# One MLP up product as seven half-size products per pair of output tiles

## The reference, cut to what matters

```python
def _sq_relu_mlp(x, w1, w2):
    return jnp.square(jax.nn.relu(x @ w1)) @ w2     # w1 (1024, 4096), w2 (4096, 1024)
```

## Time and profile before

| what | us |
|---|---|
| median of 3 runs | 2175.79 |
| the runs | 2176.32, 2171.49, 2175.79 |
| span of the profiled execution (first to last instruction) | 2171.2 |
| its own time outside the span | not shown by the page |
| PE busy | 2118.4 (98%) |
| DVE / ACT / POOL busy | 1026.0 / 818.7 / 133.8 |
| output projection, in the chain | 538.97 to 643.5 |
| up product of layer 0 | 644.37 to 1033.26 |
| down product of layer 0 starts | 1033.26 |

### The profile page before, as it was taken

The page is one execution under the profiler, slowest core; times in us unless marked ns, Lnnn a source line. Parts: engine busy times, 40 slices in busy tenths (PEclk is TensorE's granted clock), DMA queues, the critical chain, the costliest instruction groups (busy, mean ns, idle before and its releaser), DMA issues.

```text
span 2171.2 us, 31832 instructions
## 1 busy us (share of the span) xinstructions
PE 2118.4 (98%) x13227; PEld 1912.4 (88%) x13227; DVE 1026.0 (47%) x1503; ACT 818.7 (38%) x1507; POOL 133.8 (6%) x214
## 2 busy tenths in 40 slices
PE   7999999999999999999999999999999999999998
PEld 7999877777789999999888878789999999888886
DVE  5120287566553333333645467663333335444475
ACT  5111397545332223232523245452222224333343
POOL 1000131000110000000000013220000000000011
PEclk9999999999999999999999999999999999999999
DMA  5331301098426666665876553436666566665464
GB/s 172 87 86 36 141 26 34 19 406 329 141 80 225 219 225 217 220 212 217 283 246 228 170 163 98 144 128 229 228 216 226 212 219 235 240 224 169 161 216 137
DMA packets 205963, 394.21 MB, mean 182 GB/s; under 512 B 18749, under 2 KB 100853, under 8 KB 197500
## 3 DMA queue, kind: packets, MB, share of 16 engines
q1 hardware_dynamic: 199628, 387.45, 51.6%
q10 hardware_dynamic: 6192, 4.72, 0.7%
HBM read 273.12 MB, written 119.24 MB: 181 GB/s over the span
## 4 chain that ended last, share of the span: by engine, by line
PE 76%; DVE 2%; ACT 1%; issue 1%; POOL 0%; DMA 0%; POOLq 0%; DVEq 0%; SPq 0%; ACTq 0%
PE ps L1914 34%; PE ps L1953 27%; PE ps L3097 4%; PE ps L1971 3%; PE ps L1413 2%; PE ps L1923 1%; PE ps L3017 1%; PE ps L1434 1%; PE ps L1474 1%; PE ps L2990 1%; PE ps L1455 0%; DMA t_b_raw<-scratch_t_ops 0%; PE ps L3117 0%; PE ps L3030 0%; POOL stats L1529 0%
## 5 line engine op out<-in xcount | busy, mean ns | idle before, releaser
L1953 PE MATMUL ps<-t_b_hi,t_a_hi 128*128 128x512 f32 x896 | 351.7, 393 | 2.1 <-DVE t_y L1823 1.1
L1953 PE MATMUL ps<-t_b_lo,t_a_hi 128*128 128x512 f32 x896 | 348.9, 389 | 0.0
L1953 PE MATMUL ps<-t_b_hi,t_a_lo 128*128 128x512 f32 x896 | 348.9, 389 | 0.0
L1914 PE MATMUL ps<-m_xT_hi,t_w_lo 128*128 128x384 f32 (+1 forms) x1480 | 326.7, 328 | 0.0
L1914 PE MATMUL ps<-m_xT_lo,t_w_hi 128*128 128x384 f32 (+1 forms) x1480 | 326.7, 328 | 0.0
L1914 PE MATMUL ps<-m_xT_hi,t_w_hi 128*128 128x384 f32 (+1 forms) x1480 | 326.7, 328 | 0.0
L1680 DVE TENSOR_TENSOR t_w_lo<-t_raw,t_w_hi 128x1024 fp32r<-128x1024 f32 x64 | 78.3, 1225 | 427.0 <-ACT t_w_hi L1676 427.0
L1744 DVE TENSOR_TENSOR t_a_lo<-t_a_raw,t_a_hi 128x1024 fp32r<-128x1024 f32 x112 | 137.2, 1225 | 300.3 <-ACT t_a_hi L1737 300.3
L1737 ACT ACTIVATE t_a_hi<-t_a_raw 128x1024 fp32r<-128x1024 f32 x112 | 118.8, 1061 | 396.3 <-PE ps L1971 275.8
L1676 ACT ACTIVATE t_w_hi<-t_raw 128x1024 fp32r<-128x1024 f32 x64 | 67.7, 1058 | 504.9 <-PE ps L1914 492.2
L1914 PEld LDWEIGHTS ps<-m_xT_hi,t_w_lo 128*128 128x128 f32 x1480 | 252.9, 188 | 0.0
(11 more groups left out here) (284 smaller groups left out, 3010.2 us busy)
## 6 DMA issues: line engine op xcount, KB each, us to landing
scratch_t_ops<-t_t SPq DMA_DIRECT2D x32, 1280.0 KB, 5.5
scratch_s_ops<-t_s SPq DMA_DIRECT2D x32, 1280.0 KB, 4.5
t_a_raw<-scratch_s_ops SPq DMA_DIRECT2D x80, 512.0 KB, 3.9
t_b_raw<-scratch_t_ops SPq DMA_DIRECT2D x80, 512.0 KB, 4.7
t_raw<-mlp_w SPq DMA_DIRECT2D x64, 512.0 KB, 4.1
t_w_raw<-mlp_w SPq DMA_DIRECT2D x32, 1024.0 KB, 7.7
scratch_a_ops<-t_h SPq DMA_DIRECT2D x32, 512.0 KB, 5.5
t_a_raw<-scratch_a_ops SPq DMA_DIRECT2D x32, 512.0 KB, 3.4
```

Source lines behind the costliest of these rows:

```text
L1914: mm = self.nc.tensor.matmul(out, a[:, k, :], b_[:, k, c], start=(k == 0 and x == 0), stop=(k == KT - 1 and x == 2))
L1953: mm = self.nc.tensor.matmul(self.core.ps[:, self.BANK[idx] + tp, :], a[s][:, kk, tp * P:(tp + 1) * P], w[s][:, kk, :], start=(c == 0 and ...
```

## The change: what it does, and the diff

`m0` becomes `SevenUp`, a subclass of `Mlp`. For pair i the 1024 x 256 weights are a 2x2 of blocks (two contraction halves, two column tiles), the 1024 x 1088 tokens a 2x2 of contraction halves and token halves (544 each: 512 prompt tokens and 32 sample tokens). Seven block products (P1 to P7) of 4 contraction tiles x 3 passes x 2 chunks of 272 columns replace the eight of a plain product: 24 matmuls each, 168 per pair.

- Sums of weights (4 per pair, 128x512 each) are made by POOL (`sum_weights`); sums of tokens (four, once) by POOL for tiles 0, 4, 1, 5, 2, 6 and the samples (`sum_tiles`, in the output projection's steps), by DVE for tiles 3 and 7.
- Token tiles come in the order 0, 4, samples, 1, 5, 2, 6, 3, 7. Each transposed tile is taken twice by ACT: `hi` as before and an unsplit copy into a staging area.
- The split of the token sums (`sum_split_hi`, `sum_split_lo`, twelve of each) stands in ACT's and DVE's lists around and behind the last tile; the first nine products are interleaved with it.
- Sums of products stay in PSUM: P2 adds onto P1's bank, P7 and P4 onto P6's, P3 onto P5's; DVE takes a partial sum out (`take_out`) before the next product is added to the bank, so those products wait for it.
- Products are split and multiplied in a fixed `ORDER`, weight splits run 3 ahead in a ring of 6 slots.
- `one_s`, `one_t` and `one_w2` are single buffers where there were two.
- Several semaphores are merged (the loads of `w_out` into two groups, gains, residuals).

```diff
+def product_order():
+    return ([(i, x) for x in (1, 2) for i in range(2)] + [(i, x) for i in range(2) for x in (6, 7, 5, 4, 3)]
+            + [(i, x) for i in range(2, PAIRS) for x in (1, 6, 2, 7, 5, 4, 3)])
+    TAKEN_AFTER = {P6: U2, P7: U3, P5: C22, P4: C21, P3: C12}
+    def load_w2(self, sp, i):
+        if i == 0:
+            sp.wait_ge(self.sum_lo_done, 12)
+        else:
+            sp.wait_ge(self.t_ready, i)
...
+    def up_loads(self, sp):
+        self.load_w2(sp, 0)
+        for i in range(PAIRS):
+            if i == 1:
+                sp.wait_ge(self.w_summed, 8)
+                self.load_e0(sp, 3)
+            elif i + 2 < PAIRS:
+                sp.wait_ge(self.multiplied, self.done(i, self.P2))
+                self.load_e0(sp, i + 2)
+            if i == 0:
+                sp.wait_ge(self.multiplied, self.done(1, self.P2))
+                self.load_e0(sp, 1)
+            self.store_t(sp, i)
+            if i + 1 < PAIRS:
+                self.load_w2(sp, i + 1)
+            if i + 2 < PAIRS:
+                sp.wait_ge(self.multiplied, self.done(i, self.P4))
+                self.load_e1(sp, i + 2)
+            if i + 1 < PAIRS:
+                self.store_s(sp, i)
+    def sum_weights(self, pool, i):
+        if i >= 2:
+            pool.wait_ge(self.multiplied, self.done(i - 2, self.P3))
+        self.wait_e0(pool, i)
+        self.wait_e1(pool, i)
+        add(s1, a21, a22, ALU.add).then_inc(self.w_summed, 1)
+        pool.wait_ge(self.w_summed, n + 1)
+        add(s2, s1, a11, ALU.subtract).then_inc(self.w_summed, 1)
+        add(a21, a11, a21, ALU.subtract).then_inc(self.w_summed, 1)
+        pool.wait_ge(self.w_summed, n + 2)
+        add(s4, a12, s2, ALU.subtract).then_inc(self.w_summed, 1)
+    def act_step(self, act, p):
+        i, x = self.ORDER[p - 1]
+        if x == self.P1:
+            self.copy_first(act, i)
+        elif x == self.P2:
+            self.take_c11(act, i)
+        if p + self.AHEAD < self.PRODUCTS:
+            self.w_split_hi(act, p + self.AHEAD)
+        if x in (self.P5, self.P4, self.P3):
+            self.finish_block(act, i, self.TAKEN_AFTER[x])
+    def dve_step(self, dve, p):
+        i, x = self.ORDER[p - 1]
+        if x in self.TAKEN_AFTER:
+            self.take_out(dve, i, x)
+        if p + self.AHEAD < self.PRODUCTS:
+            self.w_split_lo(dve, p + self.AHEAD)
+        if p < self.PRODUCTS and self.ORDER[p][1] == self.P7:
+            self.combine_t(dve, self.ORDER[p][0])
+        if self.ORDER[p - 2][1] == self.P3:
+            self.combine_s(dve, self.ORDER[p - 2][0])
+    def wait_place(self, pe, i, x):
...
+        elif x == self.P2:
+            pe.wait_ge(self.first_copied, i + 1)
+        elif x == self.P7:
+            pe.wait_ge(self.added, 5 * i + self.U2)
...
+        elif x == self.P4:
+            pe.wait_ge(self.added, 5 * i + self.U3)
+        else:
+            pe.wait_ge(self.added, 5 * i + self.C22)
@@ gpsimd, output projection @@
             for j in range(3, NT):
                 out_post.root(core, pool, j)
+                if j == NT - 2:
+                    m0.sum_tiles(pool, 3)
                 out_pre.root(core, pool, j)
+                if j == 3:
+                    m0.sum_weights(pool, 0)
+                if 3 <= j <= 4:
+                    m0.sum_tiles(pool, j - 3)
+                if j == 6:
+                    m0.sum_tiles(pool, 2)
+            m0.up_pool(pool)
@@ vector, end of the output projection @@
+            take_out_lo(NT - 2)
+            add_y(NT - 1)
+            m0.sum_split_lo(dve, 2, 0, 0)
+            m0.sum_split_lo(dve, 2, "s", 1)
+            m0.w_split_lo(dve, 3)
+            mlp_input(NT - 1)
+            m0.sum_split_lo(dve, 4, 0, 2)
+            m0.w_split_lo(dve, 4)
             take_out_lo(NT - 1)
+            m0.sum_last_tiles(dve, 0)
+            m0.sum_split_lo(dve, 2, 1, 3)
+            m0.w_split_lo(dve, 5)
...
+            m0.dve_up(dve)
@@ tensor, end of the output projection @@
             turn_out(NT - 2)
+            pe.wait_ge(out_post.scaled, NT - 1)
+            pe.wait_ge(m0.x_lo_done, 6)
+            pe.wait_ge(m0.w_lo_done, 1)
+            m0.product(0, (0,))
+            pe.wait_ge(m0.w_lo_done, 2)
+            m0.product(1, (0,))
+            pe.wait_ge(m0.x_lo_done, NT - 1)
+            m0.product(0, (1,)).then_inc(m0.multiplied, 1)
+            m0.product(1, (1,)).then_inc(m0.multiplied, 1)
+            m0.multiply(pe, 2)
+            turn_out(NT - 1)
+            m0.multiply(pe, 3)
+            pe.wait_ge(m0.sum_lo_done, 4)
+            m0.multiply(pe, 4)
+            pe.wait_ge(m0.sum_lo_done, 7)
+            m0.multiply(pe, 5)
...
```

More of the change, by code:

```diff
@@ L1584, in __init__ @@
         self.xT_hi, self.xT_lo = xT_hi, xT_lo
[L1585 to L1590, removed]
+        self.up_semaphores(core, tag)
         self.s_ready = core.sem(tag + "s_ready")
@@ L1606, in __init__, with up_semaphores @@
         self.sample_taken = core.sem(tag + "sample_taken")
+    def up_semaphores(self, core, tag):
+        self.raw_in = [core.sem(f"{tag}raw_in{s}") for s in range(2)]
+        self.hi_done = core.sem(tag + "hi_done")
+        self.lo_done = core.sem(tag + "lo_done")
+        self.up_ready = core.sem(tag + "up_ready")
+        self.relu_done = core.sem(tag + "relu_done")
+        self.hidden_done = core.sem(tag + "hidden_done")
     def load_w1(self, sp, n):
@@ L2000, in down @@
                 between(g, tp)
+class UpMap:
+    HALF = TOK // 2
+    A_HI = 0
+    A_LO = A_HI + KT * HALF * 4
+    B_HI = A_LO + KT * HALF * 4
+    B_LO = B_HI + KT * HALF * 2
+    WEIGHTS_EVEN = B_LO + KT * HALF * 2
+    RING = WEIGHTS_EVEN + 7 * 2048
+    WEIGHTS_ODD = RING + 6 * 2048
+    FIRST = WEIGHTS_ODD + 7 * 2048
+    SUM = KT * HALF * 4
+    SUM_3 = 101376
+    SUM_2 = SUM_3 + SUM
+    SUM_1 = SUM_2 + SUM
+    SUM_4 = SUM_1 + SUM
+    H = SUM_4 + SUM
+    SAMPLES = H + 2 * 4 * HALF * 4
+    S = SAMPLES + 2 * PAIRS * NS * 4
+    W2 = S + 10 * 1024
+    T = W2 + 8 * 1024
+    END = T + 10 * 1024
@@ L2021 @@
     b_lo: list = field(default_factory=list)
-OUT_TILES = [0, 1, PT] + list(range(2, PT))
+OUT_TILES = [0, PT // 2, PT] + [t + half for t in range(1, PT // 2) for half in (0, PT // 2)]
 def trunk(core, sample, qT, qT_offset, xT_hi, xT_lo, ins, gains, tables, x_in, x1, x3, operands, outs):
@@ L2470, in split_w_out @@
             def split_w_out(i):
-                act.wait_ge(wo_in[i], 16 * len(w_out_pieces(i)))
+                group = range(W_OUT_EARLY) if i < W_OUT_EARLY else range(W_OUT_EARLY, KT)
+                act.wait_ge(wo_in[int(i >= W_OUT_EARLY)], 16 * sum(len(w_out_pieces(x)) for x in group))
                 if i == 0:
@@ L2525, in _ @@
             square_x1(2)
-            for j in range(3, NT):
+            for j in range(3, NT - 1):
                 act.wait_ge(out_pre.squared, j)
```

501 lines of the change are left out of this document (434 added, 67 removed).

## The result

| | us |
|---|---|
| before, median (range), 4 runs on the same chip | 2173.9 (2171.5 to 2176.3) |
| after, median (range), 4 runs | 2222.4 (2220.7 to 2223.6) |
| ratio after / before | 1.0228, 95% interval 1.0213 to 1.0242 |
| profiled span before, after | 2171.2, 2218.9 |
| predicted | 2185, range 2152 to 2211 |

The account below looks back on a forecast made before the run. PE was taken to bound the kernel, busy 98%. Stage: 342 work + 25 idle + 3 clock = 370, plus 27 of stalls, 397 to 398 against 389.8; carried to the median, 2185 us, range 2152 to 2211.

Parts of the forecast that it names:

- The price of a matmul: Up product: a 272-column matmul costs 0.1267 us, bounds 0.120 and 0.128; a pair takes 21.3 us instead of 24.0.
- steps (a) to (g): Stage start: PE's waits step by step, from late norm roots to pair 1's second weight load; with pair 1, 25 us idle.
- the first copy: Stage start: P2 waits for copy_first, behind the square of x1 on ACT and add_y on DVE; PE idle 3.4 us.
- before P6: Stage start: after its transpose, tile 7 must be taken twice, split, summed and its sum split; PE idle 2.9 us.
- before P7: Pair 0: P7 waits for U2, behind eight sum splits, one add and three weight splits on DVE; PE idle 7.7 us.
- (f) and (g): Pair 0: P4 waits for U3 behind the w2 load, idle 3 to 4 us; P3 for pair 1's weight work, 2.
- rivals 1 and 2: Steady pairs: POOL's adds do not hold DVE, 2157, chance 0.28; or ready DVE instructions go first, 2165, chance 0.12.
- rival 1: Steady pairs: DVE is not held by POOL's adds, stalls vanish and 19 us stay gained: 2157, chance 0.28.
- load for POOL's sums: Steady pairs: load issued at T-3.04 lands 4.0 us later, sums start about T+1.2; T is the end of P3.
- rival 3: Steady pairs: stalls also lower the clock, 1.8 us for each of 14 pairs, 25 more: 2210, chance 0.10.
- the down product's first step: End of the stage: the down product finds its operands as before, hidden by the last product; no added time.
- stall of one pair, 14 times: Steady pairs: POOL's adds and DVE take turns, so U2 is late and P7 waits 1.9 us; 27 us for 14.

Follow-up runs that it names:

- experiments 1 and 5: Changed kernel with GpSimd's weight sums of pairs 2 to 15 left out, 2170.3 us; changed kernel with those sums made by VectorE instead, 2174.5 us.
- experiment 8: Changed kernel with weight sums from pair 1 on VectorE, late weight load first, combine_t behind C22, start and end reordered: 2142.6 us; norm roots also earlier: 2142.9.
- experiment 6: Changed kernel with the second weight tile's load for the pair after next issued before the store of t and the load of w2: 2207.3 us.
- experiment 3: Changed kernel with the store of t of pair 15 put behind the first two operand loads of the down product: 2219.0 us.
- experiment 9: First kernel of experiment 8 with the first down-product operands split before C21 of pair 15 and combine_t(15) back before U3: 2141.7 us.
- x10: Kernel with weight sums of pairs 2 to 15 on VectorE, with combine_t moved ahead of U2 from pair 2 on: 2204.5 us.
- x11: As x10, but with only three of combine_t's four sums ahead of U2: 2200.7 us.

## Why the prediction was right in kind and wrong in size

**Right.**
- The price of a matmul: 0.1254 us apart (23 distances from 863.43 to 869.20 at two a row) beside 0.1267 predicted. A pair's work is 21.07, not 21.3.
- The start: P3 of pair 0 begins at 694.97, about 3 us later than my steps (a) to (g) give (692), and all of that is the later end of the output projection; from there the steps give 48 us and it took 48.2. That is in part luck: the gaps were 3 us shorter than summed, 19.4 for 22.4, and a lower clock (0.90 from 646.94 to 694.97) made up for it. Each gap stands where a step put it: 2.9 at the first copy (3.4), 2.7 before P6 (2.9), 6.3 before P7 (7.7), 5.0 before P3 in place of (f) and (g), 2.5 in pair 1 (2 to 3).
- DVE and POOL exclude each other, and a ready DVE does not go first: rivals 1 and 2 fall. This was less well founded than it read. The earlier trace rows show POOL held, but not that it got in between two instructions of VectorE, whose next one began 0.04 us after the last while POOL's was not yet through; that the two take turns only the changed kernel shows.
- Where the sums are away (experiments 1 and 5) the kernel stands at the time of before, not at rival 1's 2157: 8 us more go at the end, and 0.6 a pair at P4 (the gap of 0.39 and the 0.2 until the last matmul ahead of it has ended: 21.67 against the 21.05 of experiment 8, both at clock 1.00), of which the cheaper matmul gives 3 back.

**Wrong: four terms.** The change costs 48.5 us (2222.4 - 2173.9), where my terms give 397.5 - 389.8 = 7.7; 40.8 are to be explained. (The 2185 has two slips on top: the sum says 8 to 9 and adds 9, and 2175.8 was 1.9 above the median of before as it stands now.)

| term | predicted | measured | us |
|---|---|---|---|
| load for POOL's sums | 4.2 from issue to first sum, at T+1.2 | 5.9, T+3.1; in experiment 6 4.8, T+2.0 | 15.1 (experiment 6) |
| clock behind the steady gaps | none (rival 3: 25, chance 0.10) | in experiment 6 over all 14 pairs | 13.5 |
| the down product's first step | "as before, hidden" | gap 6.1, and its first 216 matmuls 50.8 instead of 49.0 | 8 |
| stall of one pair, 14 times | 1.9 | in experiment 6 a gap of 2.1 and 0.2 until the matmul ahead of it has ended | 6 |
| output projection, start, price of a matmul | | | -3 |

They sum to about 40, 1 less than the difference.

The step that failed first is "weights whose load is issued at P4's end (T-3.04) and lands 4.0 later". The 4.0 is the landing time in a kernel that issues this load 8.7 us after the one of w2, when that has landed. The changed kernel issues it some 6 us after, while w2 is still on its way (10.6 us to landing instead of 7.7). I had the new order of SyncE's list and the times of its waits before me, and said of the loads only that the buffers had time. They had; the start of POOL's sums had not. Experiment 6 moves the load ahead of them and gets sums at T+2.0 and P7 2.3 us late. For sums at T+2 the prediction's own working gives 2.7, and for T+1.2, which one pair of the changed kernel nearly meets (T+1.3, gap 1.57), 1.8. So the model of the two engines taking turns was right to half a microsecond, and its input wrong.

Rival 3 was held at 0.10 because the gap of the earlier trace rows was longer than a steady one; that a gap of 2 us costs 1.5 us of clock in some of the pairs no row of before could show. In the changed kernel the clock takes 25.60 - 21.28 - 2.98 = 1.34 us a pair, 16 over the 14 pairs, two thirds of that rival's 25.

The third term was put at nothing without a look at the lists. SyncE's list puts the store of t 15, which waits for `combine_t` (done at 1065.3), ahead of the first operand loads:

```profile
1064.75 0.61 DVE u_t L2445
1065.37 0.02 issue
1065.38 0.33 SPq L2167
...
1065.90 0.37 SPq L1653
...
1066.31 8.63 DMA t_b_raw<-scratch_t_ops
...
1074.96 1.06 ACT t_a_hi L2544
...
1077.19 1.23 DVE t_b_lo L1749
1078.42 0.04 issue
1078.47 50.79 PE ps L1955 x216
```

That order is only a part of it: with the store out of the way 2.5 of the 6.1 us stay, for the splits that stand behind C21 (experiment 3), and experiment 9 removes these.

## What to carry to other kernels

GpSimd may look free and still hold up the critical path, where its reads of SBUF meet VectorE instructions with two SBUF inputs: 5 us of its sums cost PE 4.5 us in each pair, idle and at a lower clock, and the same sums on the "busier" VectorE cost PE nothing. When a step moves, take a load's landing time from what goes out ahead of it after the move, and how long before, not from its old median, and walk every queue to the end of the stage. Gaps of PE of 1.9 us and more cost more than their length here, in some of the pairs 1.5 us of clock on top; those of 0.4 (experiments 1 and 5) did not. So a stall is worth removing altogether: with nearly all of them gone the same seven products are 1.4% faster than the kernel before (0.986), where they were 2.3% slower.

## What the runs showed of the hardware

- VectorE and GpSimd instructions that both take two inputs from SBUF alternate, one whole instruction each, when both lists are full: 2309 ns for 1215, 1917 for 1280. Memsets of GpSimd beside VectorE's sums stretch nothing (1218), and neither do GpSimd's sums a VectorE instruction whose second input is in PSUM (720 at most, for 715).
- Behind equal gaps of 1.95 us the same 168 matmuls take 21.28 or 22.8 us, nothing between, and the granted clock is low (0.65) only in the first few us behind the gap. Behind gaps of 3.76 us none of 12 pairs kept the clock.
- Granted clock and idle time must be read together: x10 and x11 differ by 0.6 us a pair in their gaps, 8 us in all, and by 3.8 in time, as the kernel with the shorter gap lost the clock more often (5 of 13 pairs, not 2).
- The landing time of a load depends on what was issued ahead of it and how long before: 512 KB behind a store of 1280 KB and a load of 1024 KB take 3.9 to 4.4 us when they are issued 8.7 us after that load (the kernel before), 5.7 us (median) when 3.6 to 7.6 us after it (the changed one), and 4.6 when they go out ahead of both (experiment 6).
